# The last mixer iteration rebuilt: sample rows ahead of the last prompt tile's output product

## The reference

```python
mod = silu(c) @ w_ada + b_ada              # shift, scale, gate for mixer and channel mixer
h = rmsnorm(x, g_mix) * (1 + sc_m) + sh_m
a, b, q, k, v, g = split(h @ w_in)         # six groups of 512 columns
glu = a * sigmoid(b)
conv = silu(layernorm(causal_depthwise_conv31([state_conv, glu])))
o = retention(rotary(q), rotary(k), v, state_ret)   # 4 heads of 128; returns the new state too
x = x + gt_m * (concat[conv, groupnorm(o) * silu(g)] @ w_out)
h = rmsnorm(x, g_ffn) * (1 + sc_f) + sh_f
x = x + gt_f * (shared_expert(h) + sum over the top 6 of 64 experts, weighted)
y = rmsnorm(x, g_final)
```

## Time and profile before

| | |
|---|---|
| Time, median of 3 runs | 1590.01 us (1589.7 to 1591.05) |
| Profiled execution: time / span | 1590.49 us / 1588.7 us |
| Mean granted TensorE clock | 0.958 of 2.4 GHz |
| PE busy | 1444.5 us, 91% |
| DVE busy | 845.3 us, 53% |
| POOL busy | 494.7 us, 31% |
| ACT busy | 213.0 us, 13% |
| HBM read / written | 323.09 MB / 62.62 MB |

### The profile page before, as it was taken

One profiled execution on the slowest core, in us unless ns is written; L12 is line 12 of the kernel. 1 busy time (PEld: TensorE's weight loads), 2 busy tenths in 40 slices (PEclk: granted clock), 3 DMA queues, 4 the chain that ended last, 5 costly groups with the idle time before them and its releaser, 6 DMA issues.

```text
span 1588.7 us, 17546 instructions
## 1 busy us (share of the span) xinstructions
PE 1444.5 (91%) x5851; PEld 653.0 (41%) x5851; DVE 845.3 (53%) x2135; ACT 213.0 (13%) x358; POOL 494.7 (31%) x426
## 2 busy tenths in 40 slices
PE   4899999999999999988799998999979999999947
PEld 2344454555545455554343332344423333333313
DVE  1147778998988999575533323333333232333317
ACT  1111231312222231222000000000000000000003
POOL 0001010121211111304545444454544545454410
PEclk9999999999999999958799999999999999999978
DMA  9987211211120000603399999999999999999975
GB/s 333 329 316 266 96 43 67 82 40 70 40 83 27 32 29 27 189 33 114 119 369 326 344 370 360 364 373 364 373 366 358 375 363 374 353 368 360 372 219 239
DMA packets 93690, 370.17 MB, mean 233 GB/s; under 512 B 17763, under 2 KB 29447, under 8 KB 68461
## 3 DMA queue, kind: packets, MB, share of 16 engines
q1 hardware_dynamic: 69637, 304.77, 49.5%
q0 software_dynamic: 23968, 64.35, 16.2%
HBM read 323.09 MB, written 62.62 MB: 243 GB/s over the span
## 4 chain that ended last, share of the span: by engine, by line
DMA 37%; PE 30%; DVE 19%; issue 7%; SPq 4%; ACT 2%; POOL 1%; POOLq 0%; DVEq 0%; ACTq 0%
DMA acc_rows<-W,kT 17%; DMA acc_rows<-xr,kT 15%; PE U L649 9%; PE R L702 8%; DVE cv L1188 7%; PE U L831 5%; PE R L847 2%; SPq L396 2%; DMA W<-in_w_ada 2%; DMA acc_rows<-xr,shared_f 1%; DMA W<-h_rows,q_r 1%; PE R L613 1%; SPq L403 1%; PE U L673 1%; PE U L757 1%
## 5 line engine op out<-in xcount | busy, mean ns | idle before, releaser
L649 PE MATMUL U<-W,hT 128*128 128x512 f32 x864 | 386.2, 601 | 1.2 <-issue 1.2
L1188 DVE SCALAR_TENSOR_TENSOR cv<-win,cw,cv 128x128 f32<-128x128 f32 x960 | 254.8, 344 | 1.4
L831 PE MATMUL U<-W,cat 128*32 128x512 f32 (+2 forms) x1072 | 239.0, 614 | 5.8 <-issue 3.7
L831 PE MATMUL U<-W,hT 128*32 128x512 f32 (+2 forms) x976 | 237.9, 608 | 6.0 <-issue 6.0
L847 PE MATMUL R<-W,glu 128*32 128x512 f32 (+2 forms) x1024 | 240.8, 597 | 1.3 <-DVE glu L1458 1.3
L649 PEld LDWEIGHTS U<-W,hT 128*128 128x128 f32 x864 | 162.5, 193 | 189.0 <-issue 189.0
L1445 DVE STREAM_TRANSPOSE cat<-W 128x1024 f32<-128x1024 f32 x33 | 67.4, 2042 | 203.0 <-DMA W<-h_rows,q_r 200.1
L1445 DVE STREAM_TRANSPOSE hT<-x_t 128x1024 f32<-128x1024 f32 x33 | 67.3, 2039 | 189.5 <-DMA x_t<-h_rows,q_r 168.0
L847 PEld LDWEIGHTS R<-W,glu 128*32 128x32 f32 (+2 forms) x1024 | 84.1, 138 | 150.8 <-issue 149.3
L831 PEld LDWEIGHTS U<-W,hT 128*32 128x32 f32 (+2 forms) x976 | 88.5, 144 | 131.2 <-issue 129.7
L831 PEld LDWEIGHTS U<-W,cat 128*32 128x32 f32 (+2 forms) x1072 | 85.4, 139 | 135.1 <-issue 130.9
(11 more groups left out here) (252 smaller groups left out, 1189.9 us busy)
## 6 DMA issues: line engine op xcount, KB each, us to landing
W<-in_w SPq DMA_DIRECT2D x192, 1024.0 KB, 17.6
W<-in_w_ada SPq DMA_DIRECT2D x24, 1024.0 KB, 8.7
W<-in_w_in SPq DMA_DIRECT2D x6, 2048.0 KB, 19.9
W<-acc_rows SPq DMA_DIRECT2D x16, 512.0 KB, 9.5
x_rows<-xr SPq DMA_DIRECT2D x9, 512.0 KB, 3.3
h_rows<-xr SPq DMA_DIRECT2D x9, 512.0 KB, 2.7
x_t<-in_x_prompt SPq DMA_DIRECT2D x8, 512.0 KB
W<-in_w_out SPq DMA_DIRECT2D x1, 4096.0 KB, 17.4
```

The lines of the kernel that those rows point to most:

```text
L649: last = mm(U[BANK[g]][:, :], hT[:, k, :], w_in[:, k, 512 * g:512 * g + 512], start=k == 0, stop=k == KT - 1)
L831: last = mm(U[1][cols, :], xgT[z][:, k, cols], w13[:, :, k, :], start=k == 0, stop=k == KT - 1)
L1188: ins = v.scalar_tensor_tensor(cv[:, c, :], win[:, c, w:w + P], cw[:, c, w:w + 1], cv[:, c, :], ALU.mult, ALU.add)
```

## The change

The last iteration is taken out of `body` and written by itself on every engine, in another order. On TensorE and VectorE the sample rows' retention and conv come first, then `mix_out` of tile 7, then the sample's w_out product on eight rows (`cat_s`, eight columns as the stationary side), then route of tile 7 and the state products, with the shared expert's first products between them. The new state is now made wholly on TensorE (the old state goes in through a product with the identity), and ScalarE copies it back with the decay as a scale; ScalarE also makes the masked v rows. The sample's residual, norm and router work on 8 rows. The stored conv inputs come in the layout that the conv needs, channel by partition, so they are loaded by one DMA and not transposed; the array is laid out so on the host. SP stores the sample's rows after the new states. On POOL the orders of gathers and list writes change. `AHEAD` goes from 5 to 4, and with it the order of executions and of experts. `-` and `+` mark lines of before and after; other places only lose the `prompt` branches.

```diff
-AHEAD = 5
+AHEAD = 4
...
-        sconv = late[:, 0:2, 1024:1024 + DC]
+        sconv = late[:, 2, 1024:1024 + CT * NS * CW]
...
+        cat_s = maskT[:, 1, 0:KT * NS].rearrange("p (k b) -> p k b", k=KT)
+        xs, hs = mods[0:NS, 1, :], xr[0:NS, :]
+        k_s = k_d[0:NS, :]
+        cross_s, logits_s = X[0:NS, 0:512].rearrange("p (h n) -> p h n", h=H), X[0:NS, 512:512 + NE]
...
             sp.wait_ge(uk_done, NT)
+            sp.dma_start(sconv, t["state_conv_t"]).then_inc(sconv_in, 16)
...
+            sp.dma_start(xs, t["x_sample"][:, 0, :]).then_inc(xr_in, 16)
...
+            sp.wait_ge(x2_ready, NT)
+            sp.dma_start(x2_rows[SEQ:TOKENS, :], xs).then_inc(x2_stored, 16)
+            sp.wait_ge(h2_ready, NT)
+            sp.dma_start(h2_rows[SEQ:ROWS, :], xr[:, :]).then_inc(h2_stored, 16)
+            sp.wait_ge(newret_out, 16 * (NS + 1))
...
+                at = slice(512 * (n % 2), 512 * (n % 2) + 512)
+                mm(R[:, at], k_s[:, P * h:P * h + P], vmask[:, 2 * half:2 * half + 2, :, P * h:P * h + P], start=True, stop=False)
+                mm(R[:, at], ident[:, :], S0[:, 2 * half:2 * half + 2, :, h, :], start=False, stop=True).then_inc(state_mm, 1)
...
+            def few_rows(src, bank, done):
+                for c in range(4):
+                    last = tr(bank[:, c, 0:NS], src[0:NS, P * c:P * c + P], ident[0:NS, 0:NS])
+                last.then_inc(done, 1)
+
+            def few_sum(src, done):
+                for c in range(CT):
+                    last = mm(T0[:, 0:NS], mean_w[:, :], src[:, c, 0:NS], start=c == 0, stop=c == CT - 1)
+                last.then_inc(done, 1)
+
+            positions(TP - 3, pick, TP)
...
+            few_rows(q_r, T4, q_posed)
...
+            for h in range(H):
+                for b in range(NS):
+                    last = mm(U[0][:, h * NS + b:h * NS + b + 1], S0[:, b // 2, b % 2, h, :], qT[:, h, b:b + 1], start=True, stop=True)
+            last.then_inc(s_cross_done, 1)
+            pe.wait_ge(crossT_ready, 1)
+            pe.wait_ge(hT_ready, NT)
+            pe.wait_ge(h2T_ready, TP - 1)
+            for h in range(H):
+                last = tr(cross_s[:, h, :], crossT[:, h, :], ident[:, :])
+            last.then_inc(cross_posed, 1)
+            pe.wait_ge(conv_ready, NT)
+            few_sum(cv, sum1_done)
...
+            mix_out(TP - 1)
...
+            few_sum(sq, sum2_done)
+            pe.wait_ge(ret_ready, NT)
+            pe.wait_ge(score_ready, TP - 1)
+            pe.wait_ge(dest_ready, TP - 2)
+            few_rows(o_t[:, :, :].rearrange("p h e -> p (h e)"), R24, ret_posed)
+            pe.wait_ge(catA_part, 4 * NT)
+            pe.wait_ge(catB_ready, NT)
+            pe.wait_ge(k_rot, NT)
+            for n in range(2):
+                for k in range(KT):
+                    last = mm(U[n][0:NS, :], cat_s[:, k, :], w_out[:, k, 512 * n:512 * n + 512], start=k == 0, stop=k == KT - 1)
+            last.then_inc(wout_done, 1)
+            pe.wait_ge(sret_ready, 1)
+            rows2_trans(TP - 1, hT_ready, NT)
+            pe.wait_ge(vmask_ready, 1)
+            state_product(0)
+            state_product(1)
+            router(TP - 1, TP)
+            state_product(2)
+            state_product(3)
+            pe.wait_ge(score_ready, TP)
...
+            pe.wait_ge(x2_ready, NT)
+            up(0, shw_all, 0)
+            pe.wait_ge(h2_ready, NT)
+            for k in range(KT):
+                last = tr(Xk[:, k, 0:NS], hs[:, P * k:P * k + P], ident[0:NS, 0:NS])
+            last.then_inc(h2_posed, 1)
+            for n in range(H, 2 * H):
+                state_product(n)
+            pe.wait_ge(h2T_ready, NT)
+            for k in range(KT):
+                last = mm(logits_s, h2T[:, k, 0:NS], w_rt[:, k, :], start=k == 0, stop=k == KT - 1)
+            last.then_inc(router_done, 1)
+            hidden_trans(0)
+            up(1, shw_all, 1)
             pe.wait_ge(state_upd, 2 * H)
-            pe.wait_ge(h2T_ready, TP)
-            up(0, shw_all, 0)
-            rows2_trans(TP, hT_ready, NT)
-            hidden_trans(0)
-            pe.wait_ge(dest_ready, TP)
-            router(TP, TP)
-            up(1, shw_all, 1)
+            positions(TP - 1, pick, NT)
             down(0, shw_all)
             positions(TP, pick_s[:, :], NT)
             hidden_trans(1)
...
+            nc.scalar.activation(qT[:, :, 0:NS], T4[:, :, 0:NS], ACT.Copy).then_inc(qT_ready, 1)
...
+            for h in range(H):
+                cols = slice(HD * h, HD * h + HD)
+                nc.scalar.activation(k_s[:, cols], k_r[0:NS, cols], ACT.Copy, scale=1.0 / GAMMA[h])
+            for b in range(NS):
+                last = nc.scalar.activation(vmask[:, b // 2, b % 2, :], v_t[0:NS, :], ACT.Copy, scale=ident[0:NS, b:b + 1])
...
+            def state_update(n):
+                h, half = n // 2, n % 2
+                act.wait_ge(state_mm, n + 1)
+                nc.scalar.activation(S0[:, 2 * half:2 * half + 2, :, h, :], R[:, 512 * (n % 2):512 * (n % 2) + 512].rearrange(
+                    "p (k c e) -> p k c e", k=2, c=2), ACT.Copy, scale=float(GAMMA[h])).then_inc(state_upd, 1)
+
+            state_update(0)
+            state_update(1)
+            score(TP - 1)
+            state_update(2)
+            state_update(3)

...
+            def sample_tail():
+                place(TP - 3, pick, TP)
+                link(v.tensor_tensor(qk_prod, q_r[:, :].rearrange("p (h d) -> p h d", h=H),
+                                     k_r[:, :].rearrange("p (h d) -> p h d", h=H), ALU.mult))
...
+            def sample_residual():
+                halves = [slice(512 * n, 512 * n + 512) for n in range(2)]
+                dve.wait_ge(wout_done, NT)
+                dve.wait_ge(smod2_in, 16)
+                for n in range(2):
+                    ins = v.tensor_tensor(U[n][0:NS, :], U[n][0:NS, :], gt_m[0:NS, halves[n]], ALU.mult)
+                ins.then_inc(y_gated, 1)
+                dve.wait_ge(y_gated, NT)
+                dve.wait_ge(xr_in, 16 * NT)
+                for n in range(2):
+                    ins = v.tensor_tensor(xs[:, halves[n]], U[n][0:NS, :], xs[:, halves[n]], ALU.add)
+                ins.then_inc(x2_ready, 1)
+                dve.wait_ge(x2_ready, NT)
+            def sample_norm2():
+                dve.wait_ge(norm2_std, NT)
+                link(v.reciprocal(rstd2[0:NS, :], std2[0:NS, :]))
+                dve.wait_ge(smod3_in, 32)
+                dve.wait_ge(h2T_ready, TP)
+                link(v.scalar_tensor_tensor(X[0:NS, :], xs, rstd2[0:NS, :], A_f[0:NS, :], ALU.mult, ALU.mult))
+                dve.wait_ge(h2_posed, TP)
+                dve.wait_ge(h2_stored, 16 * TP)
+                v.tensor_tensor(hs, X[0:NS, :], B_f[0:NS, :], ALU.add).then_inc(h2_ready, 1)
+                dve.wait_ge(h2_ready, NT)
...
-            xpose(0)
-            residual(TP)
-            norm2(TP)
-            place(TP - 1, pick, NT)
+            sample_tail()
+            residual(TP - 1)
+            norm2(TP - 1)
+            top_k(TP - 2)
+            sample_residual()
+            place(TP - 2, pick, NT)
+            sample_norm2()
+            top_k(TP - 1)
             blk_hid(0)
             blk_hidT(0)
             dve.wait_ge(router_done, NT)
             xpose(1)
+            place(TP - 1, pick, NT)
             top_k(TP)
...
+            gather(0)
             fill_list(TP - 3)
-            gather(0)
             ret_out(TP)
+            gather(1)
             fill_list(TP - 2)
-            gather(1)
+            fill_list(TP - 1)
             gather(2)
-            fill_list(TP - 1)
+            fill_list(TP, NS)
             gather(3)
-            fill_list(TP, NS)
             pool.wait_ge(spare_in, 16 * 10)
             scatter(0)
-            gather(4)
             scatter(1)
             pool.wait_ge(slot_ready, 2)
+            gather(4)
...
+    taps = np.pad(arrays["state_conv"][0], ((0, 0), (0, 1), (0, 0))).reshape(NS, CW, CT, P)
+    arrays["state_conv_t"] = np.ascontiguousarray(taps.transpose(3, 2, 0, 1).reshape(P, CT * NS * CW))
```

More of the change, by code:

```diff
@@ L430, in load_residual @@
                     sp.wait_ge(h2_posed, j)
[L431 to L434 removed]
+                sp.dma_start(xr[:, :], t["x_prompt"][0][bass.ds(j * P, P), :]).then_inc(xr_in, 16)
             store_mod(0)
@@ L707, in body @@
                 j, m = i - 1, i - 2
-                prompt = not (isinstance(j, int) and j == TP)
                 if tail:
@@ L721, in body @@
                     project(i, GA, ua_done, k_rot, i)
-                if tail and prompt:
+                if tail:
                     pe.wait_ge(kT_ready, j + 1)
@@ L789, in body @@
                     project(i, GK, uk_done, q_rot, i + 1)
-                if tail and not prompt:
-                    for n in range(H, 2 * H):
-                        state_product(n)
                 if tail:
@@ L1278, in place @@
                 dve.wait_ge(dest_ready, m + 1)
-            def state_update(n):
```

(14 more changed lines are left out.)

186 lines of the change are left out of this document (86 added, 100 removed).

## The result

The changed kernel took 1592.93 us (median of 20 runs, 1587.82 to 1598.64), the kernel before 1589.4 (20 runs, 1585.03 to 1595.56): a ratio of 1.0021, 95% interval 1.0011 to 1.0031. It is slower by 3.5 us by the medians, where 1.5 us less was forecast. The profiled execution has a span of 1592.8 and a time of 1594.62, granted clock 0.957.

What follows compares the result with a forecast made beforehand. It took the known line of experts and the first routed product to start one train of serial scatters, transfers and matmuls nearly balanced. Early stage -5.4, AHEAD +3.9: 1590.49 - 1.5 - 0.48 = 1588.5; own range 1585 to 1592, overall 1577 to 1598.

Steps and rivals of the forecast that it cites:

- TensorE's run up to the second shared product: Early stage on TensorE: 26.8 from the sample's output product to 733.8, then gate and handoffs to 740.6.
- the 64 passes: One-column passes of the sample's attention on TensorE, priced 11.75 as in the old order, from 658.1 to 669.9.
- the output product of tile 7: TensorE after the sample's attention, from 672.7: 13.95 with the clock up, 15.57 if it must rise; 15.57 taken.
- the sample's output product: TensorE's 32 passes for the eight sample rows, priced 13.95 to 15.57, taken 14.7, ending at 707.0.
- the eight state products: TensorE's new sample state, four 512-column passes each at 0.44, 1.74 a product, 13.9 in all, at full clock.
- The line at 779.9: Time when the line of experts is known and expert weights can start: forecast 772.4, 8.1 earlier than 780.5.
- a sign of being wrong: The prediction would be wrong if the line of experts was known before 766 or after 778.
- the first routed product: Upward product of the first routed execution on TensorE: forecast near 813.2 as execution 4, 5.4 earlier than 818.65.
- the two weight stalls: TensorE's waits for expert weights: one expected to go, 7.5 taken, leaving the AHEAD move at net +3.9.
- the transfers set the end: Rival: the full DMA share limits the expert phase, so the end moves by -6.7 to 1583.3; chance 0.27.
- Its extra for a clock that stays up: Addition to the transfers rival: clock up in the 64 passes gains 11.75 / 2 + 1.6, some 6 more, giving 1577.
- The full step of 11.4: Rival: serial scatters make the extra execution cost 11.4 with no stall removed, +6.0 to 1596.0; chance 0.23.
- the rival that the line would not be earlier: Rival: an unseen 8 us handoff, SP's sample-row store behind the state outputs, gives +6.5, 1596.5; chance 0.10.

Runs made afterwards that it cites:

- filler: Changed kernel with three unread 512-column products in TensorE's gap between the two output products: ratio 1.0042 to the kernel before.
- the kernel with six ahead: Combined kernel (changed kernel, position products first, POOL's gathers one place further ahead, five ahead) with six shared executions ahead instead: ratio 0.9992 to the kernel before.
- POOL's order: Changed kernel with POOL's third gather before tile 7's list writes and fourth before the sample's: ratio 1.0020 to the kernel before.
- the order undone: Changed kernel with tile 7's output product moved back ahead of the sample's attention on TensorE: ratio 1.0057 to the kernel before.
- that run: Filler kernel with a 128-row weight tile as stationary side of the first state product, making the sample's new state wrong: ratio 0.9976 to the kernel before.

## Why the prediction failed, by its own steps

**The step that failed is TensorE's run up to the second shared product, by the size of four terms.** Forecast and measured: the 64 passes 11.75 and 13.10; the output product of tile 7 15.57 and 16.73; the sample's output product 14.7 and 16.52; the eight state products 13.9 and 17.6 (fifteen steps of 1.04 in the mean and a last one of 1.98 at half clock). The misses are 1.35 + 1.16 + 1.82 + 3.7 = 8.0, small terms give 0.8 back, and tile 7 was placed at 759.6 where the forecast had 752.4, 7.2 later. The gap between the output products was right (4.0), so were the routers, the tables and the second shared product (8.60 for 8.57).

The first of the four misses is chance: in the twelve profiles with this order the 64 passes took 10.39 to 13.18, 11.7 in the mean, which is the forecast. The other three recur: the product of tile 7 took 15.4 to 16.9 (mean 16.5), the sample's 15.6 to 16.6 wherever no filler stood before it, and the state products 17.3 to 18.4 with eight rows and no filler.

Of the first three terms the cause is the clock. 15.57 was taken as the price of a product that starts with the clock down, and as the upper bound: but the row it came from the earlier trace rows is a product in which the clock was back at 1.00 after 3.3 us, where in the changed kernel it took 5.5. All that started at 0.50 took 15.4 to 16.9 here, so 15.57 lies near the lower end. And the sample's product was priced between full clock and that, though the forecast itself put a wait of 4 ahead of it. The fourth term took its price from another shape: 0.44 a pass is that of products with 128 rows on the stationary side. The old state product, also with eight rows, stood in the trace of before, at a granted clock of 0.50:

```profile
712.46 3.78 PE L673 MATMUL U<-W,k_r 8*128 8x512 f32 x4
```

That is 0.945 for each of four passes, against 0.87 for a dense pass at that clock (an estimate, twice 13.95 / 32). It would have shown a price above the dense one, if not the size; I had not read it.

**Behind that, the queues did as forecast, 7 us late.** The line at 779.9 is past 778, which the prediction had named as a sign of being wrong. Six list writes 7.6 (forecast 7.7), the third gather's last issue 4.0 behind its first (4.0), from there to the transposition 2.8 (2.5), from that to the known line 4.9 (4.9), the sample's writes 7.1 (7.2). Two terms missed and nearly cancelled: the fourth gather was used 7.2 behind its last issue and not 10.7, but the first routed gather's last issue stood 7.0 behind the slot rows and not 4.3, since the second scatter stood ahead of it. So the first routed product is 819.9 where 813.2 was forecast. (The forecast's landing of that gather, 810.6, has a slip of 0.4: 800.3 and 10.7 are 811.0.)

**AHEAD 5 to 4 was right by the profiles**: +3.9 forecast, +2.8 in the profiled execution, +4.1 as a mean over the kernels with either, +4.0 in whole time when done alone. One of the two weight stalls went, as expected: all ten kernels with four ahead have one such wait of TensorE (3.0 to 6.7; 3.05 in the changed kernel), all four with five have two (9.8 to 10.5 together; 9.8 before). And from the scatter of the first routed execution (844.72) to the last one (1537.19) it is 61 steps of 11.35, as forecast. In the changed kernel whole times put 6.4 on the move and leave the early stage a gain of 3.0 (1.0 to 4.9) where 5.4 was forecast. That the early stage fell short holds by both readings; how the miss divides between the two steps in a typical execution stays open.

**The rivals.** That the transfers set the end is not what happened: the windows show 358 GB/s and a share of 1.01 (359 and 1.01 before, in the same window), and still the rest followed the number of executions left (773.5 with four ahead, 769.4 with five), and from the known line to the end it was anything from 807.8 to 819.8, the longest in the kernel with six ahead and the earliest line. The Trainium skill's rule (DMA: Bandwidth & Descriptors, "Where 436 GB/s comes from", some 358 GB/s for a core) agrees with the rate in the trace; the sum that I hung on it does not follow. (Its extra for a clock that stays up is 7.5 by the terms given, not 6; the clock did not stay up.) The full step of 11.4 was not paid either, since a stall went. Nearest came the rival that the line would not be earlier; but SP's queue, which was its mechanism, stands nowhere in the waits between 657 and 780: the delay is TensorE's.

## What to carry to other kernels

Price a pass by a row of its own shape and its own clock, and where a dense product follows a wait or thin passes, take the longest row of one that started with the clock down, since such rows differ by 1.5 us here. Before a change that shortens a chain, look for the short instructions that feed the next queue and stand behind long ones: half a microsecond of position products held POOL, and moving them ahead was worth 10 us, three times what the change lost. A wait taken out of a queue (POOL's order) gave nothing while the next wait in the same queue, a scatter for the rows of the one before, ended later.

## What the runs showed of the hardware

Where passes with eight rows on the stationary side alternate with 128-row passes, both take 0.53 at full clock; with 128 rows in all of them they take 0.43. The Trainium skill (TensorE: Matmul & The Clock Gate, "Why this matters for your kernels") says that a product over 32 rows takes the same time as over 128; for this alternation the runs measure 1.23 times as much. Eight columns on the stationary side cost nothing (13.90 for 32 passes, 13.95 with 128).

The granted clock fell to 0.50 with TensorE busy without a gap, in the eight-row state products: in the changed kernel at the last of them (the pair at 737.08 took 2.06), with the filler at 728, with the order undone at 734 (busy 22.00 of 22.00 us ahead of it). With 128 rows it held to their end, which speaks against the rival of that run. The Trainium skill (TensorE: Matmul & The Clock Gate, "Why this matters for your kernels") names idle gaps between bursts as what makes the throughput drop; these falls had none ahead of them in the stretch that the windows show. What decides it I have not isolated.
